# Segments of 128, 128, 256, 256, 256 and 64 tokens with separate row streams, and a token shift scaled by ScalarE's evictions

## The reference

```python
h = layer_norm(x)
p = h @ w_in                     # 1792 RWKV columns, 1536 attention columns
pm = p + (prev(p) - p) * mu      # token shift: prev is the row of the token before
# RWKV-7: r, k, v = pm[...]; a = sigmoid(a0 + al @ a2)
#   k = k * (1 + (a - 1) * k_a); a recurrence over the tokens, 8 heads of 64
# differential attention: causal by chunks of 64 tokens, 4 heads
m = concat(rwkv, attention) @ w_out
h = layer_norm(alpha * h + m)
q = h @ wq                       # 8 heads; top 16 of 128 keys twice, then top 16 of the pairs
idx, gate = top16(q, subkeys)    # 128 rows of the tables for each token
f = sum_e gate_e * gelu(u_tab[idx_e] . h) * v_tab[idx_e]
h = layer_norm(alpha * h + f)
```

## Time and profile before

| what | value |
|---|---|
| median of 3 runs | 4201.76 us (lowest 4198.4) |
| profiled execution | 4201.42 us |
| its span, first to last instruction | 4199.6 us |
| busy: PE, DVE, POOL, ACT | 2858.0, 2419.6, 2387.5, 671.8 us |
| mean granted TensorE clock | 0.803 of full speed |
| moved by DMA | 1325.36 MB, 316 GB/s over the span |

### The profile page before, as it was taken

The page is one execution under the profiler, slowest core; times in us unless marked ns, Lnnn a source line. Parts: engine busy times, 40 slices in busy tenths (PEclk is TensorE's granted clock), DMA queues, the critical chain, the costliest instruction groups (busy, mean ns, idle before and its releaser), DMA issues. The chain is left out here.

```text
span 4199.6 us, 48966 instructions
## 1 busy us (share of the span) xinstructions
PE 2858.0 (68%) x18591; PEld 1580.0 (38%) x18591; DVE 2419.6 (58%) x5633; ACT 671.8 (16%) x1913; POOL 2387.5 (57%) x2194
## 2 busy tenths in 40 slices
PE   7887376787746777768567777667545666675566
PEld 5666354445413343446134343344112222330011
DVE  3427977565864555667855555569745465673311
ACT  3331122220011122101012222101011111000000
POOL 0001366665455665675765665665666776676764
PEclk9988677888977787879788987789767767687788
DMA  3125688889788988899998897998999999999997
GB/s 110 69 67 208 226 303 312 313 332 385 288 324 317 347 289 315 331 374 351 352 371 304 336 339 285 338 374 313 373 378 356 360 383 359 388 373 349 370 365 297
DMA packets 371523, 1325.36 MB, mean 316 GB/s; under 512 B 40188, under 2 KB 75416, under 8 KB 360152
## 3 DMA queue, kind: packets, MB, share of 16 engines
q0 software_dynamic: 314576, 1145.45, 72.7%
q1 hardware_dynamic: 56712, 176.79, 11.2%
HBM read 1310.53 MB, written 11.29 MB: 315 GB/s over the span
## 5 line engine op out<-in xcount | busy, mean ns | idle before, releaser
L752 POOL DMA_INDIRECT ring_u<-in_peer_u,idx x1088 | 1222.6, 1124 | 1088.3 <-DVE gates L1703 396.0
L1460 DVE CUSTOM_DVE_ANT_0 ring_u<-ring_u,h 128x1024 f32<-128x1024 f32 x1088 | 1294.2, 1224 | 568.3 <-DMA ring_u<-in_peer_u,idx 447.3
L752 POOL DMA_INDIRECT ring_v<-in_peer_v,idx_t x1042 | 1114.2, 1069 | 686.5 <-PE pacc L1110 347.9
L1110 PE MATMUL pacc<-ring_v,spread_w 128*32 128x512 f32 x4168 | 1029.2, 737 | 470.6 <-DMA ring_v<-in_peer_v,idx_t 343.0
L1110 PEld LDWEIGHTS pacc<-ring_v,spread_w 128*32 128x32 f32 x4168 | 170.5, 121 | 1050.5 <-DMA ring_v<-in_peer_v,idx_t 686.3
L1085 PE MATMUL pm<-arena 64*64 64x64 f32 (+1 forms) x6256 | 375.8, 257 | 273.8 <-issue 147.1
L1071 PE MATMUL pm<-hT,wts 128*128 128x256 f32 (+2 forms) x2656 | 544.9, 365 | 25.1 <-issue 14.0
L1071 PEld LDWEIGHTS pm<-hT,wts 128*128 128x128 f32 x2656 | 465.0, 208 | 144.6 <-issue 78.0
L1085 PEld LDWEIGHTS pm<-arena 64*64 64x64 f32 x6256 | 295.5, 157 | 434.7 <-issue 251.2
L1071 PE MATMUL pm<-wts,hT 128*128 128x384 f32 (+1 forms) x576 | 201.3, 504 | 7.5 <-DMA wts<-in_sets 7.4
L1071 PE MATMUL pm<-wts,mixT 128*128 128x128 f32 (+1 forms) x1152 | 148.2, 283 | 13.1 <-DVEq L541 5.1
(11 more groups left out here) (223 smaller groups left out, 2708.2 us busy)
## 6 DMA issues: line engine op xcount, KB each, us to landing
wts<-in_sets SPq DMA_DIRECT2D x82, 1536.0 KB
ring_u<-in_peer_u,idx POOLq DMA_INDIRECT x1088
ring_v<-in_peer_v,idx_t POOLq DMA_INDIRECT x1042
wts<-in_sets SPq DMA_DIRECT2D x11, 1024.0 KB
arena<-in_subkeys SPq DMA_DIRECT2D x5, 1024.0 KB
arena<-in_x_prompt SPq DMA_DIRECT2D x8, 512.0 KB
out<-arena SPq DMA_DIRECT2D x64, 64.0 KB
out<-h POOLq DMA_DIRECT2D x8, 512.0 KB
```

The costliest lines, as they stand in the source:

```text
L752: pool.indirect_dma_start(out=out, out_offset=None, in_=table, in_offset=bass.IndirectOffsetOnAxis(ap=index.bitcast(U32), axis=0)).then_in ...
L1110: x = pe.matmul(pacc[out, c, :], spread_w[:, blocks % 2, quad, place % EIGHTH, :], row[:, c * 512:(c + 1) * 512], start=(place == 0), stop ...
L1460: v.tensor_tensor_reduce(ring_u[:, row, :], ring_u[:, row, :], h1[:, g % 4, :], 1.0, 0.0, ALU.mult, ALU.add, dots[:, slot:slot + 1]).then_ ...
```

## The change

The segments become 128, 128, 256, 256, 256 and 64 tokens, each with one closing (`passes` is one list of all tiles; `closed` and `closing` lose their second part; `FIRST_ROUND` goes). There are six mixings and 108 weight sets, where there were five and 99. A round is no longer "u of tile g beside v of tile g - 1" from end to end: a stream opens and closes by itself (`u_open`, `u_close`, `v_open`, `v_close`, in place of `open` and `close`), and a table says which rows go beside which part of a segment's mixing. So segment 1 has tile 0's u rows beside it and then 80% of its v rows, with no u rows; segment 2 has tile 1 in the same way. From segment 4 on the table gives what the rounds gave before.

The token shift is made by linearity: ScalarE writes `mu * p` for the row ahead and `(1 - mu) * p` for the row itself (two evictions of the same PSUM row, each with a scale that is one number per partition), and VectorE adds them, one instruction in place of two. The factor of k, `1 + (a - 1) * k_a`, moves from VectorE (L1531) to ScalarE.

```diff
-        self.first_tile = n * NT
+        self.first_tile = first_tile
-        self.passes = [[t] for t in range(self.tiles)] if n == 0 else [list(range(self.tiles))]
+        self.passes = [list(range(self.tiles))]
-SEGMENTS = [Segment(i, False, i * SEG, SEG) for i in range(SEQ // SEG)] + [Segment(SEQ // SEG, True, 0, DEC)]
+SEGMENTS = [Segment(0, False, 0, P, 0), Segment(1, False, P, P, 1), Segment(2, False, SEG, SEG, 2), Segment(3, False, 2 * SEG, SEG, 4),
+            Segment(4, False, 3 * SEG, SEG, 6), Segment(5, True, 0, DEC, 8)]
...
+ROUNDS = {
+    1: [(0.48, u_rows(0), []), (0.52, [], v_rows(0, 0.0, 0.8))],
+    2: [(0.46, u_rows(1), v_rows(0, 0.8, 1.0)), (0.54, [], v_rows(1, 0.0, 0.8))],
+    3: [(0.48, u_rows(2), v_rows(1, 0.8, 1.0)), (0.52, u_rows(3), v_rows(2))],
+    4: [(0.50, u_rows(4), v_rows(3)), (0.50, u_rows(5), v_rows(4))],
+    5: [(0.50, u_rows(6), v_rows(5)), (0.50, u_rows(7), v_rows(6))],
+}
...
-            def copy_row(row, src, s, c, full):
+            def shifted_row(dst, row, src, s, c, full):
                 kept, w = prev[:, 1 if s.sample else 0, c:c + 1], s.width
-                tl.link(act.activation(row[:, 0:1], kept, ACT.Copy))
+                tl.link(act.activation(row[:, 0:1], kept, ACT.Copy, scale=par[:, MU + c:MU + c + 1]))
                 tl.next(S[full])
                 act.activation(kept, src[:, w - 1:w], ACT.Copy)
-                return act.activation(row[:, 1:1 + w], src, ACT.Copy)
+                act.activation(row[:, 1:1 + w], src, ACT.Copy, scale=par[:, MU + c:MU + c + 1])
+                return act.activation(dst, src, ACT.Copy, scale=keep_mu[:, c:c + 1])
...
-                        act.activation(a_t[:, 0:w], pm[:, 2, 0:w], ACT.Sigmoid, bias=par[:, A0 + j:A0 + j + 1]).then_inc(S["lo_sig"], 1)
+                        tl.told(act.activation(a_t[:, 0:w], pm[:, 2, 0:w], ACT.Sigmoid, bias=par[:, A0 + j:A0 + j + 1]), S["at_ready"])
+                        act.activation(delta[:, 0:w], a_t[:, 0:w], ACT.Identity, bias=one_minus_ka[:, j:j + 1], scale=par[:, KAW + j:KAW + j + 1]).then_inc(S["delta_ready"], 1)
...
-                        tl.next(S["lo_sig"], 3)
+                        tl.next(S["lo_sig"], 2)
+                        tl.next(S["at_ready"])
...
-            def shift(dst, src, w, mu, tmp):
+            def shift(dst, row, w):
-                tl.link(v.tensor_tensor(tmp[:, 0:w], src[:, 0:w], src[:, 1:w + 1], ALU.subtract))
-                tl.link(v.scalar_tensor_tensor(dst, tmp[:, 0:w], mu, src[:, 1:w + 1], ALU.mult, ALU.add))
+                tl.link(v.tensor_tensor(dst, dst, row[:, 0:w], ALU.add))
...
-                        tl.next(S["lo_sig"], 2)
-                        tl.link(v.tensor_scalar(delta[:, 0:w], a_t[:, 0:w], par[:, KAW + j:KAW + j + 1], one_minus_ka[:, j:j + 1], ALU.mult, ALU.add))
+                        tl.next(S["lo_sig"])
+                        tl.next(S["delta_ready"])
```

More of the change, by code:

```diff
@@ L91, in main_steps @@
         steps += [("rwkv", s, j), ("levels", s, j), ("chunks", s, j)]
-    return steps + [x for part in closing(s) for x in part]
+    return steps + closing(s)
 def closing(s):
[L97 to L100, removed]
+    return [("project", s, 0), ("norm", s, 0), ("query", s, 0)] + [("topk", s, t) for t in range(s.tiles)]
 def pass_number(s, i):
@@ L132, in merged, with closed @@
             out += [y for y, at in zip(a, places) if at == i]
[L133 to L147, removed]
+    return out + closed(s)
+def closed(s):
+    both = stage("project", 1, [("main", "project", s, 0), ("main", "norm", s, 0)])
+    out = both[0] + both[1] + stage("query", 1, [("main", "query", s, 0)])[0]
+    for t in range(s.tiles):
+        out += stage("topk", s.tiles, [("main", "topk", s, t)])[0]
     return out
@@ L244, in spread, with alternate @@
     assert not left_u and not left_v
[L245 to L252, removed]
+    return order
+def alternate(us, vs):
+    opened, us = us[:1], us[1:]
+    started, vs = vs[:1], vs[1:]
+    out, n = started + opened, BESIDE if us else 0
     for i in range(n):
         out += vs[2 * i:2 * i + 2] + us[i * len(us) // n:(i + 1) * len(us) // n]
-    return [("open", g, None)] + out + vs[2 * n:] + [("close", g, None)]
+    return out + vs[2 * n:]
+ROUNDS = {
[5 more added lines that the diff above has]
+}
 def ring_homes():
@@ L276, in plan @@
     order = [("mix", None, x[0]) for x in merged(SEGMENTS[0])]
[L277 to L284, removed]
+    for s in SEGMENTS[1:]:
+        mixes = merged(s)
+        share, at, done, upto = [x[1] / sum(y[1] for y in mixes) + x[2] / sum(y[2] for y in mixes) for x in mixes], 0, 0.0, 0.0
+        for part, us, vs in ROUNDS[s.n]:
+            end, upto = at, upto + 2.0 * part
+            while end < len(mixes) and (upto > 1.99 or done < upto):
+                done += share[end]
                 end += 1
-            order += spread(g, mixes[at:end])
+            order += spread(mixes[at:end], us, vs)
             at = end
     for g in range(SEGMENTS[-1].first_tile, len(TILES) + 1):
-        order += alternate(g)
+        order += alternate(u_rows(g) if g < len(TILES) else [], v_rows(g - 1))
     return order
@@ L897, in mixing @@
                         for x, bank in RAW:
[L898 removed]
+                            shifted_row(rkv[:, x, 0:w], raw[:, x, :], pm[:, bank, 0:w], s, 4 * x + j, "raw_full").then_inc(S["raw_read"], 1)
                         enter(act, "act", kind, s, j)
@@ L1115, in extra @@
             def extra(kind, g):
-                if kind == "open" and g > 0:
-                    rows = TILES[g - 1][0].rows
-                    if g > 1:
-                        pe.wait_ge(S["f_read"], g - 1)
-                    pe.wait_ge(S["weight_ready"], g)
-                    if folds(g - 1) == 1:
+                if kind == "v_open":
+                    rows = TILES[g][0].rows
+                    if g > 0:
+                        pe.wait_ge(S["f_read"], g)
+                    pe.wait_ge(S["weight_ready"], g + 1)
+                    if folds(g) == 1:
                         x = pe.transpose(pacc[:, 0, 0:rows], wgt[0:rows, :], ident[0:rows, 0:rows])
@@ L1518, in mixing @@
                             tl.next(S["raw_read"])
-                            c = 4 * x + j
-                            shift(rkv[:, x, 0:w], raw[:, x, :], w, par[:, MU + c:MU + c + 1], delta)
+                            shift(rkv[:, x, 0:w], raw[:, x, :], w)
                             if x == 1:
```

97 lines of the change are left out of this document (47 added, 50 removed).

## The result

The changed kernel takes 4290.41 us (median of four runs, 4264.13 to 4309.89). The kernel before, run with it, takes 4210.88 (the median of four with a single run of 11586.56 us, which is left out of the ratio). The ratio is 1.0195 with a 95% interval of 1.0108 to 1.0282: the change makes the kernel slower by about 2%; the interval leaves out any loss under 1% and doesn't say on which side of 2% it is. The profiled execution took 4304.73 us (span 4302.9), against 4201.4 before.

What follows compares the result with a forecast made beforehand. Neither transfers nor the mixing chain alone was taken to bound the stages, transfers being the larger. 4201.4 + (2147 - 12 - 2083) up to segment 3's end - 8 behind it gave 4245 us, range 4114 to 4320.

Steps and rivals of the forecast that it cites:

- the forecast's own case: Whole kernel: the early start is paid back by one more mixing; 4180 to 4290 us, chance 0.6.
- the token shift: VectorE loses about 43 us, ScalarE gains some 9 a segment; 20 us gained, 12 before segment 4, 8 after.
- The start: Segment 0 halved to 128 tokens: a pair takes 40 us, first gather at 288 us, 111 earlier.
- rival 2: Thin matmuls lose TensorE's clock: 45 us in segment 0, some 25 in segment 1, total 4315 us; chance 0.15.
- The stages behind the start: First gather to end of segment 3: 467, 616 and 766 us, with 10 between segments 1859, before 1684.
- transfers are the larger: Segments 1 and 2 of before: neither transfers nor mixing chain alone bounds the stages, but transfers take more time.
- the rule: Stages beside gathers: time is the larger of transfers and mixing plus 0.25 (pairs) or 0.12 (closings) of the smaller.
- Rival 1: After the start transfers alone bound, so the early start stays gained except 44 us: 4114 us; chance 0.15 with half-way cases.
- Rival 3: Stretches with v rows alone in segments 1 and 2 overlap badly, 96 us more: 4341 us; chance 0.1.
- rival 4: The token shift's part does nothing or less, since VectorE is not the end: 4265 us; no separate chance given.
- Behind segment 3: Rest of the kernel: rounds, sets and waits as before, 2117 us less 8 from the token shift.

Runs made afterwards that it cites:

- whole rounds: Changed kernel with rounds rearranged in segments 1 to 3 so v rows never stand alone: 3900.97 us, 1.0187 of the kernel before.
- shift_only: Kernel before, its segments and streams kept, with only the new token shift: 3831.06 us, 0.9994 of the kernel before.
- light_sets: Changed kernel loading only the first 128 columns of segment 1's 18 weight sets, 16.8 MB less: 3944.08 us, 1.0279 of the kernel before.
- before_quarter: Kernel before, gathering 1 KB of each table row in place of 4 KB, instructions unchanged: 4158.95 us, 0.9892 of the kernel before.

## Why the prediction was right or wrong

The forecast was 4245 us with a range of 4114 to 4320; 4290 is inside and 45 above, at the very edge of the forecast's own case (4180 to 4290). The profiled execution, 4304.7 us, is 59 above: 48 up to the end of segment 3 (2195 for 2147), 12 of the token shift that did not come there, and 1 less behind it. That end was to come at 2100 to 2180 us, so this sign was missed.

- **The start.** Forecast 288 us, measured 308.3. Four pairs of about 43 and not 40 us are 12 of the 20, and embed and tails the other 8. (The working had a slip: by its own rows 7.17 less two times 1.95, or 3.3 us, and not 3.6 go from two raw rows.) The step that failed is the scaling: half the matmuls went, but they also ran at a lower clock. The masks' and grams' matmuls (line 1098, 64x128) behind a wait for VectorE took 2.40 us for 24 of them in after, where 48 took 2.43 before; a second query-key-value tile used to fill that wait. The clock of the stretch is 0.79 where it was 0.88, just above the 0.78 from which rival 2 was to decide, so it took a part and not the whole.
- **The clock after that.** Rival 2's other half, 25 us in segment 1, did not come. The clock there is 0.64 beside u rows, the lowest of all, but those 239 us were forecast as 246, since TensorE was busy only 115 of them. By the Trainium skill (page "TensorE: Matmul & The Clock Gate", section "HAM oscillation") thin matmuls with waits between their bursts are throttled again and again. The trace agrees that they are: cut into slices of 4 us, the granted clock of after goes 1.00, 0.59, 0.56, 1.00 from 84 to 100 us, the low ones in and right behind the 5.37 us for which TensorE waited for VectorE, and the same comes back in the next pair (1.00, 0.64, 0.51, 1.00 from 128 to 144 us). The four pairs lost 12 us against the forecast, waits included, and the whole start 20, where the rival had 45 in segment 0 and 70 in all.
- **The stages behind the start.** Segment 1: 448 us for 467, u part 239 for 246, the rest 209 for 221. Segment 2: 651 for 616. The closing with v rows was right (192 for 194), the pairs with v rows too (112 for 119), the u part not (347 for 303). Segment 3: 788 for 776 with the 10 us between segments. Altogether the third segment ends at 2195 where 2147 was forecast: 20 from the start, -19, +35 and +12 from the segments.
- **The step that is wrong in kind, though the sum came near,** is "transfers are the larger". I took M, the mixing with nothing beside it, as 1067 us for the middle of before (101, 463, 503) and D, the transfers of its two segments, as 1383. The engines alone, with the rows' own arithmetic, need 1360 (third device). The quarter rows say the same from the other side: with a quarter of the gathered bytes M would have been the larger in every stage, and the middle should have fallen to some 1160 us, an estimate by the rule from the prediction's rows; it took 1691 us where it had taken 1684. The likely reason, argued and not tried by itself (without gathers the engines' work was seen on the other kind of device alone), is that my M left out that VectorE and TensorE work the rows in the same program order as the mixing, so that the share of 0.87, which I read as "D nearly full", was rows queued behind engines that came late. The rule fitted four stages by construction, with two free parts (within 9 us, and not the 7 that the text says: 454 for 445 and 266 for 258). That the sum came near is owed to this fit on stages that held the engines' work already, and not to the mechanism; with the errors of the stages going both ways, part of it is luck.
- **Rival 1** (transfers bound all) is wrong for that reason. **Rival 3** (v-only stretches overlap badly, 96 us) did not come as it was put: segment 1's v part took 209 us and segment 2's 304, where the rule gave 221 and 313 and the rival 252 and 378. The rounds with v rows alone do cost, 81 us against the whole rounds on the first device. But that cost stood in the forecast by the rule (67 us for the same move), and shows in the shares of 0.55 and 0.73, for which the forecast had said 0.65.
- **The token shift** was given 20 us and is worth none (rival 4, 4265), as far as the first device tells; it did not run by itself on one of the slower kind. Both busy times were right, 43 us less of VectorE and 9 us a segment more of ScalarE; "beside gathers worth between 0 and all, I take half" was the wrong choice between the bounds. Without it the forecast would have been 4265.
- **Behind segment 3:** 2108 us for 2109, where 8 us of gain were counted on the token shift. On the first device the stretch is 22 us longer in after than in `shift_only`, so the match to 1 us is no proof of the 8; `h1` and the new waits cost nothing that shows on the device of the result. The line with the add stands 84 times, as said.

The additional 44 us for sets and constants stood in D, where the larger-and-a-part rule made them worth most of that; `light_sets` bears it out on the other kind of device (38), and on the slower kind it was not tried.

## What to carry to other kernels

A high DMA share does not say that bytes bound the kernel: leave the transfers out, or cut their bytes, before a gain is counted in unused transfer time. Splitting the first stage of a pipeline to start the second earlier pays only if the stage's fixed work (here waits, weight sets and a closing for each piece) is less than the start won: here, without any gather, the middle grew by 210 us where the start won 100. Work taken off an engine that is not the end of any stage (43 us of VectorE) moved the time by 0.06%, at most 0.23%.

## What the runs showed of the hardware

The same program takes about 4205 us on one device and 3834 on another. The busy times differ little (TensorE 2858 us on the slower kind, 2818 on the other). The waits differ, but not all that look so. The rows of the waits (engine, what it worked for, releaser: us in total, times, longest), before on the device of the forecast, and below them the whole idle time of the second line:

```profile
PEld pacc L1110 <- DMA ring_v<-in_peer_v,idx_t: 686.3, 369, 16.5
PEld pacc L1110 <- issue: 385.6, 596, 23.8
...
PEld pm L1085 <- issue: 285.3, 231, 15.2
...
L1085 PEld LDWEIGHTS pm<-arena 64*64 64x64 f32 x6256 | 295.5, 157 | 434.7 <-issue 251.2
```

and the same lines of `shift_only` on the first device:

```profile
PEld pacc L1112 <- DMA ring_v<-in_peer_v,idx_t: 939.7, 567, 21.1
PEld pacc L1112 <- issue: 175.9, 457, 5.5
...
PEld pm L1087 <- issue: 101.5, 159, 1.7
...
L1087 PEld LDWEIGHTS pm<-arena 64*64 64x64 f32 x6256 | 272.2, 148 | 247.6 <-issue 87.7 <-DVE arena L1547 62.4 <-ACT arena L927 26.0
```

Before the v rows' weight loads the two wait alike, 1072 us and 1116: there the slower kind has more under "issue" (waits for nothing that the profile shows) and less under the DMA, so that this row by itself shows no longer wait. Before the weight loads of the mixing's small matmuls (L1085) the idle time is really longer, 435 us for 248, with single waits under "issue" of up to 15 us where the other kind has 1.7. The two kinds differ by 370 us in all; how much of the 187 us lies on the path that ends last is not shown. The clock is 0.803 in the mean (0.848 on the other), and the share behind segment 2 is 0.93 in place of 0.99. `before_quarter` has the long waits too on such a device, with a quarter of the gathered bytes (254.4 us, longest 25.0, in the same line, which is its L1088), so they do not come from the amount moved. Their cause stays open: it wasn't tried, and no run without gathers was made on such a device. So it also stays open what paces the stretch behind segment 3 there. It is not bytes alone; a gather keeps GpSimd 0.94 us (the median of L752) and 0.30 us of issue behind it, which for 1286 gathers of a mean 1.10 us is some 1800 of 2065 us in `before_quarter`, near but not at the end. On ScalarE a scaled copy with a per-partition factor took 470 to 477 ns at 256 columns and `Identity` with two per-partition operands 602 ns, where an immediate factor takes 380.
